# Fourteen of 22 tiles of a feed-forward's down projection as seven quarter products, eight half by half

## The reference, cut to what matters

```
gu = x @ w_gu                                  # 1024 x (2*2816)
gate, up = gu[..., :2816], gu[..., 2816:]
ffn = (silu(gate) * up) @ w_down               # (1024 x 2816) @ (2816 x 1024)
x   = layer_norm(ALPHA * x + ffn, ln2_g, ln2_b)
# second layer begins: h = rmsnorm(x, g_mix_pre) * (1 + scale_m) + shift_m ; q, k, v, ... = h @ w_in_2
```

## Time and profile before

| | us |
|---|---|
| runs (3): median | 2929.09 |
| runs: lowest, highest | 2924.64, 2931.28 |
| profiled execution | 2924.11 |
| span of its profile | 2922.4 |
| mean granted TensorE clock, of full speed | 0.992 |

### The profile page before, as it was taken

One profiled execution on the slowest core, in us unless ns is written; L12 is line 12 of the kernel. 1 busy time (PEld: TensorE's weight loads), 2 busy tenths in 40 slices (PEclk: granted clock), 3 DMA queues, 4 the chain that ended last, 5 costly groups with the idle time before them and its releaser, 6 DMA issues.

```text
span 2922.4 us, 33825 instructions
## 1 busy us (share of the span) xinstructions
PE 2827.5 (97%) x12957; PEld 2090.6 (72%) x12957; DVE 1470.3 (50%) x2344; ACT 892.4 (31%) x1532; POOL 1263.0 (43%) x824
## 2 busy tenths in 40 slices
PE   8999999889999999999899988999999899999998
PEld 5444457468888888887788655677777688888886
DVE  0599977746733334152513765221421732235998
ACT  2501036531233332112311364110121444454443
POOL 2000000036777776666667302445445587753020
PEclk9999999999999999999999999999999999999999
DMA  4111136233422224545333101333344333346864
GB/s 113 29 36 37 43 96 189 87 123 117 130 87 84 82 87 135 200 141 165 108 87 101 44 1 30 86 103 122 87 116 136 123 109 115 116 158 219 280 193 173
DMA packets 349152, 327.81 MB, mean 112 GB/s; under 512 B 17984, under 2 KB 277312, under 8 KB 348992
## 3 DMA queue, kind: packets, MB, share of 16 engines
q1 hardware_dynamic: 329664, 271.13, 31.1%
q10 hardware_dynamic: 16848, 47.39, 4.2%
q0 software_dynamic: 2480, 7.13, 0.9%
HBM read 280.41 MB, written 45.19 MB: 111 GB/s over the span
## 4 chain that ended last, share of the span: by engine, by line
PE 90%; DVE 5%; issue 2%; ACT 2%; DMA 0%; POOL 0%; ACTq 0%; DVEq 0%; SPq 0%; POOLq 0%
PE PS L1343 20%; PE PS L528 19%; PE PS L1355 13%; PE PS L844 9%; PE PS L1307 5%; PE PS L1293 4%; PE PS L1578 4%; PE PS L958 3%; PE PS L1424 2%; PE PS L976 2%; PE PS L996 2%; PE PS L1535 1%; PE PS L1397 1%; PE PS L988 1%; PE PS L1438 1%
## 5 line engine op out<-in xcount | busy, mean ns | idle before, releaser
L2753 POOL TENSOR_SCALAR w_parts<-ring 128x1024 fp32r<-128x1024 f32 x198 | 231.4, 1169 | 872.9 <-PE PS L1343 258.0
L2756 POOL TENSOR_TENSOR w_parts<-ring,w_parts 128x1024 fp32r<-128x1024 f32 x198 | 513.9, 2596 | 16.5
L1343 PE MATMUL PS<-hT_high,w_parts 128*128 128x512 f32 x1312 | 433.5, 405 | 8.7 <-DVE hT_low L2360 6.4
L587 DVE TENSOR_TENSOR arena<-arena,PS 128x512 f32<-128x512 f32 x210 | 144.5, 688 | 402.5 <-PE PS L528 401.5
L1343 PEld LDWEIGHTS PS<-hT_high,w_parts 128*128 128x128 f32 x1312 | 247.3, 188 | 71.3 <-issue 11.1
L844 PE MATMUL PS<-w_parts,hid_high 128*128 128x512 f32 x896 | 276.5, 390 | 5.7 <-DVE w_parts L809 4.1
L1343 PE MATMUL PS<-hT_low,w_parts 128*128 128x512 f32 x656 | 256.2, 391 | 0.0
L1355 PE MATMUL PS<-w_parts,hid_high 128*128 128x512 f32 x704 | 218.3, 391 | 3.9 <-DVE hid_low L629 2.2
L844 PEld LDWEIGHTS PS<-w_parts,hid_high 128*128 128x128 f32 x896 | 167.7, 188 | 42.6 <-DVE w_parts L809 6.4
L528 PE MATMUL PS<-tx_high,w_parts 128*128 128x512 f32 x576 | 183.2, 389 | 0.0
L844 PE MATMUL PS<-w_parts,hid_low 128*128 128x512 f32 x448 | 174.3, 389 | 0.0
(11 more groups left out here) (345 smaller groups left out, 5621.6 us busy)
## 6 DMA issues: line engine op xcount, KB each, us to landing
ring<-in_w_in SPq DMA_DIRECT2D x112, 512.0 KB, 3.8
arena<-hid_spill SPq DMA_DIRECT2D x172, 256.0 KB, 3.7
hid_spill<-arena ACTq DMA_DIRECT2D x54, 512.0 KB, 3.1
ring<-in_w_gu SPq DMA_DIRECT2D x52, 512.0 KB, 3.9
ring<-in_w_ada SPq DMA_DIRECT2D x48, 512.0 KB, 5.2
ring<-in_w_ff SPq DMA_DIRECT2D x96, 256.0 KB, 3.3
ring<-in_w_down SPq DMA_DIRECT2D x44, 512.0 KB, 3.6
ring<-in_w_ff SPq DMA_DIRECT2D x40, 512.0 KB, 4.0
```

Source lines behind the costliest of these rows:

```text
L587: dve.tensor_tensor(out, a, self.product(g, m), ALU.add).then_inc(self.combined, 1)
L1343: mm = pe.matmul(PS[:, 2 * p + bank, :], w[:, q, k * P:(k + 1) * P], x[:, k, half_of(h)], start=(k == order[0] and n == 0), stop=(k == ord ...
L2753: pool.tensor_scalar(w_high[:, q, :], ring[:, s, :], 1.0, 1.0, ALU.mult, ALU.mult).then_inc(weights_high, 1)
L2756: pool.tensor_tensor(w_low[:, q, :], ring[:, s, :], w_high[:, q, :].bitcast(F32), ALU.subtract).then_inc(weights_used[s], 1)
```

## The change

Tiles 0 to 13 go through a second `DownSevens` (`mul1`, n_k = 7, 49 steps, products drained into y1 by `mul1.drain`); tiles 14 to 21 go through `Down` as before (REST1 = 8 steps in each half). The residual no longer rides in the add that takes the bank: `add_rows1` adds ALPHA*x1 from a second place in SBUF to y1, eight operations after step 4, and `add_down1` then adds the bank. The work of the layer norm and RMS norm of half 0 moves to other steps. Cut to its core:

```diff
+PAIRS1 = 7
+REST1 = FT - 2 * PAIRS1
...
 ORDER += ffn_order("up1", "seven1", "turn_x1", PLAIN1, SEVENS1)
+ORDER += [("prod1", p) for p in range(7)] + [("mul1", 0)]
 for half in HALVES:
-    ORDER += [("sum1", half)] + [("down1", half * FT + k) for k in range(FT)]
+    ORDER += [("sum1", half)] + [("down1", half * REST1 + k) for k in range(REST1)]
...
 PE:
             sevens1.pe(pe, 0)
+            mul1.pe(pe)
             down1.pe(pe, 0)
...
 ACT:
-            for n in range(3, 2 * FT):
+            for n in range(3, mul1.n):
+                mul1.act(act, n)
+            for n in range(2 * REST1):
                 down1.act(act, n)
-                if n == FT + 4:
+                if n == REST1 + 5:
                     ln_sqrt_half(1, 0)
-                if n == FT + 5:
                     ln_scale_half(1, 0)
-                if n == FT + 9:
-                    for b in range(4):
-                        store_x2(b)
-                        square_sum(y1[:, b, :], b, junk)
-                    sums_done(0)
-                if n == FT + 11:
-                    rms_sqrt_half(0, 0)
-                if n == FT + 13:
-                    xhat_half(0)
+            for b in range(4):
+                store_x2(b)
+                square_sum(y1[:, b, :], b, junk)
+            sums_done(0)
+            rms_sqrt_half(0, 0)
+            xhat_half(0)
...
 DVE:
+            def add_rows1(b):
+                y = y1[:, b, :].rearrange("p (a n) -> p a n", a=2)
                 dve.wait_ge(rows_back, 16 * NB)
-                dve.scalar_tensor_tensor(out=y1[:, b, :], in0=y1[:, b, :], scalar=ALPHA, in1=flat(p),
-                                         op0=ALU.mult, op1=ALU.add).then_inc(psum_free[p], 1)
+                do(dve.scalar_tensor_tensor(out=y, in0=x1_back[b], scalar=ALPHA, in1=y, op0=ALU.mult, op1=ALU.add))
...
-            for n in range(3, 2 * FT):
+            for n in range(3, mul1.n):
+                mul1.dve(dve, n)
+                if n % PAIRS1 == 3 and n > PAIRS1:
+                    mul1.drain(dve, n // PAIRS1 - 1, y1, link)
+            for n in range(2 * REST1):
                 down1.dve(dve, n)
+                if n == 2:
+                    mul1.drain(dve, 6, y1, link)
                 if n == 4:
+                    for i in range(2):
+                        mul1.drained(dve, 6, i)
+                    for b in range(NB):
+                        add_rows1(b)
                     pool_counts()
-                if n == FT + 2:
+                if n == REST1 + 3:
                     for u in range(4):
                         add_down1(0, u)
-                if n == FT + 3:
                     for u in range(4):
                         freed(dve, "sum1", 0, u)
                     ln_stats(1, 0)
-                if n == FT + 5:
+                if n == REST1 + 5:
                     ln_gain(1, 0)
-                if n == FT + 6:
+                if n == REST1 + 6:
                     ln_gain(1, 2)
-                if n == FT + 9:
-                    rms_mean(0, 0)
-                if n == FT + 11:
-                    rms_recip(0, 0)
+            rms_mean(0, 0)
+            rms_recip(0, 0)
...
 SP:
+            for n in range(mul1.n):
+                mul1.load_weights(sp, n, t["w_down"][0], slot_free)
+                mul1.load_hidden(sp, n, hidden1)
+                b, other = divmod(n - 3 * PAIRS1, 3)
+                if 0 <= b < NB and not other:
+                    sp.dma_start(x1_back[b], x1_dram[tok(b), :].rearrange("p (a n) -> p a n", a=2)
+                                 ).then_inc(rows_back, 16)
+            for n in range(2 * REST1 + 2):
+                if n < 2 * REST1:
+                    row_tile_load("down1", n, 0, t["w_down"][0], 2 * PAIRS1 + n % REST1)
                 if n >= 2:
-                    hidden1(n - 2)
-                if n == 7:
-                    sevens1.after(sp, SEVENS1, 0)
-                    for b in range(NB):
-                        sp.dma_start(y1[:, b, :], x1_dram[tok(b), :]).then_inc(rows_back, 16)
+                    down1.sp(sp, n - 2, *stored1(2 * PAIRS1 + (n - 2) % REST1))
```

More of the change, by code:

```diff
@@ L97 @@
     "seven1": (sevens(2), []),
+    "prod1": ([], ["own", "own"]),
+    "mul1": (down_steps(PAIRS1), []),
     "sum1": ([], [None, None, None, "own"]),
@@ L135 @@
             **{(stage, i): (p,) for stage in ("turn_x1", "turn_h2") for i, p in ((4, 0), (5, 3), (6, 1), (7, 0))},
-            **{("sum2", p): (2 * (p % 2), 2 * (p % 2) + 1) for p in range(7)}}
+            ("sum1", 0): (2, 3, 0, 1), ("sum1", 1): (2, 3, 0, 1),
+            **{("turn_h", i): ((i + 2) % 4,) for i in range(4)},
+            **{(stage, p): (2 * (p % 2), 2 * (p % 2) + 1) for stage in ("prod1", "sum2") for p in range(7)}}
 class Ledger:
@@ L188, in __init__ @@
                 pairs[p] += 1
-                n_units += 1
+                n_units += stage != "prod1"
         self.fulls = fulls
@@ L605, in program, with __init__ @@
         class Down:
-            def __init__(self, stage, n0, sums, n_k, sevens, hidden, back, high, low):
-                self.stage, self.sums, self.n_k, self.sevens, self.hidden = stage, sums, n_k, sevens, hidden
+            def __init__(self, stage, n0, sums, n_k, first, before, hidden, back, high, low):
+                self.stage, self.sums, self.n_k, self.first, self.before, self.hidden = stage, sums, n_k, first, before, hidden
                 self.back, self.high, self.low = back, high, low
@@ L611, in __init__, with slot @@
                 self.n0, self.split_high, self.split_low = n0, hid_high, hid_low
+                self.moved = [before.moved0[s] + before.moved_of[s] for s in range(4)]
+            def slot(self, n):
+                return (self.n0 + n) % 4
             def sp(self, sp, n, stored, value):
                 h, k = divmod(n, self.n_k)
-                self.sevens.after(sp, self.sevens.n - 1, 4)
-                if n >= 4:
-                    sp.wait_ge(self.split_low, self.n0 + n - 3)
+                sp.wait_ge(self.split_low, self.n0 + n - 3)
@@ L618, in sp @@
                 sp.wait_ge(stored, value)
-                sp.dma_start(self.back[:, n % 4, :], self.hidden[k, :, half_of(h)]).then_inc(tile_moved[n % 4], 16)
+                sp.dma_start(self.back[:, self.slot(n), :], self.hidden[self.first + k, :, half_of(h)]
+                             ).then_inc(tile_moved[self.slot(n)], 16)
             def act(self, act, n):
-                act.wait_ge(tile_moved[n % 4], 16 * ((self.n0 + n) // 4 + 2))
+                s = self.slot(n)
+                act.wait_ge(tile_moved[s], self.moved[s] + 16 * (n // 4 + 1))
@@ L636, in product @@
                     n = h * self.n_k + k
-                    return token_product(pe, L.pair(self.sums, h, u), L.part(self.stage, n, 0), self.high, self.low, n % 4,
+                    return token_product(pe, L.pair(self.sums, h, u), L.part(self.stage, n, 0), self.high, self.low, self.slot(n),
                                          slice(u * P, (u + 1) * P), k == 0, k == last)
@@ L795, in dve @@
             def dve(self, dve, n):
+                if n == 0:
+                    self.before.after(dve, self.before.n - 1, 4)
                 self.add_hidden(dve, n + 1)
@@ L905, in drain @@
                         dve.tensor_tensor(c10, c10, bank, ALU.add).then_inc(free, 1)
+                    else:
+                        self.drained(dve, 5, i)
+                        dve.tensor_tensor(c10, c10, bank, ALU.subtract).then_inc(free, 1)
             def bank_here(self, eng, u, full):
@@ L2438, in group1 @@
                 if g == SEVENS1 - 1:
-                    down1.dve(dve, 2)
+                    mul1.dve(dve, 2)
                 sevens1.sums_here(dve, g, 7)
@@ L2839, in _ @@
                 pool.dma_start(dst, t[name].to_broadcast([P, D])).then_inc(ln_rows_loaded[1], 16)
-            for n in range(2 * FT):
+            mul1.pool(pool)
+            for n in range(2 * REST1):
                 split_weights("down1", n)
```

79 lines of the change are left out of this document (46 added, 33 removed).

## The result

The changed kernel takes 2933.67 us (median of 11 runs) where the kernel before took 2925.84 in the runs made beside it; the ratio is 1.0026, 95% interval 1.0016 to 1.0036. It is slower by some 7.6 us, with 84 matmuls fewer. The profiled execution shown here is one of the longer ones: 2937.89 us, span 2936.2.

The account below looks back on a forecast made before the run. PE was taken as the bound, busy 97% of the span and 90% of the chain. Terms -19.0 + 1.0 + 9.3 + 9.7 + 6.3 = +7.3 us on 2929.1 gave 2936.4 us, range 2918 to 2945.

Parts of the forecast that it names:

- seven products themselves: Seven products of seven steps in down1: DVE's drains every 7 steps are covered, by 2 us, so PE does not wait.
- drain of product 6: Transition to the eight-tile stage: the drain frees a pair at T+3.8, block 2 wants it at T+2.7; +1.0 us.
- residual adds, step 5: Half 0: eight two-input additions alternate with POOL, 2.7 us each, delaying low part 5; stall 7.5 us, with clock +9.3 us.
- boundary: Between the halves: bank adds stand behind a later tile's low part, PE starts at X+9.7, not X+1.8; with clock +9.7 us.
- half 1: Last two steps: low part 15 queued behind ln_gain on DVE; stall 8.3, clock 1.8, less 3.8 lost before: +6.3 us.
- rows scaled for turn_h: After half 1: RMS-norm scaling ends near X+60, just when turn_h comes after two blocks; 0, at most 3 us.
- What goes: Matmuls of 14 tiles in down1: 672 become 588, so 84 x 226.7 ns go, -19.0 us however the rest falls.
- The clock: PE, after a stall of over 2 us, runs partly at the lower of 2.4 and 1.2 GHz; 1.6 to 2.0 us more.
- third rival: Products 2, 3 and 5: PE waits 3 us in each for DVE, on top of the forecast; 2946, chance 0.10.
- light lock: Residual adds and ln_gain: DVE mostly wins over POOL, additions take 1.3 us; sum -12.1, 2917 us, chance 0.18.
- Residual adds alone covered: Half 0, step 5: the residual adds cost nothing, the rest as forecast; -2.0, 2927 us, chance 0.17.
- DVE-bound products: Seven products: drains every 19 us make PE wait in products 2, 3, 5, 3 us each; 2946 us, chance 0.10.

Follow-up runs that it names:

- half of ln_gain: Changed kernel with bank adds sooner, residual adds spread, drain sooner, and ln2_b additions left out for blocks 0 to 3: ratio 0.9930 to before, 2907.89 us.
- the three moves: Changed kernel with bank adds behind REST1+2, residual adds spread over steps 4 to 7, product 6's drain behind step 1: ratio 0.9965 to before, 2916.41 us.
- residual adds spread: Changed kernel with two residual adds behind each of steps 4 to 7 of half 0, not eight behind step 4: ratio 1.0004 to before, 2927.73 us.
- sooner bank adds: Changed kernel with half 0's four bank adds behind step REST1+2 instead of REST1+3: ratio 1.0003 to before, 2926.52 us.

## Why the prediction was right

The forecast was +7.3 us, 2936.4 in a range of 2918 to 2945; measured was a ratio of 1.0026, +7.6 us, and 2933.7. Term by term, idle times from the rows above:

| term | forecast | measured |
|---|---|---|
| fewer matmuls | 84, -19.0 | 84 by the counts: 588 + 384 for 1056 |
| seven products themselves | covered | 0.4 us idle |
| drain of product 6 | stall 1.1 | 2.3 (1.8 in other runs) |
| residual adds, step 5 | stall 7.5, clock 1.8 | 5.4, clock 2.1; 6.4 us off when spread |
| boundary | stall 9.7, of which 7.9 new, clock 1.8 | 9.5, of which 7.8 new; 6.7 us off when moved (9.8 in the stage) |
| half 1 | stall 8.3, clock 1.8 | 7.2; 10 us with its clock, by half of ln_gain |
| rows scaled for turn_h | 0 | 0 |

- *What goes* held. With the three moves and half of ln_gain the ratio is 0.9930, 20.5 us off; the 84 matmuls (19.0 us) and the 3.8 us that before lost in half 1 make 22.8, and the drain's and the entry's small waits stand against it.
- *The residual adds* were right in mechanism: 20.66 us for eight, forecast 20.4. The stall was 2.1 us too long in the forecast, since PE wants step 5 later than I had it: 31.7 us after its first matmul of the eight-tile part instead of 27.2, for the drain's 2.3 us and the lower clock after them. I had priced the drain and then not carried it on. Low part 5 was late too, done after 37.0 us instead of 34.7, as the additions began 1.5 us later and the counts' small operations took 3.53 us; the two errors partly cancel.
- *The boundary* was the sharpest term, since a row of before held the very tile: 9.7 forecast, 9.5 measured. What it costs in time is less sharp: forecast 9.7 us with the clock, 6.7 by the runs and 9.8 by the stage in the profiles.
- *Half 1* was right in mechanism: ACT's root came 17.2 us after PE resumed, as forecast (1376.9 against 1359.7), and low part 15 was the late one. The two ends of it on DVE:

```profile
1376.91 0.18 DVE L2334 RECIPROCAL misc<-misc 128x4 f32<-128x4 f32 x1 [6.44 <-ACT misc L1688]
...
1400.26 0.68 DVE L648 TENSOR_TENSOR hid_low<-arena,hid_high 128x512 fp32r<-128x512 f32 x1
```

  The four pairs of ln_gain took 5.15, 5.29, 4.55 and 5.23 us, 20.2 in all, where the forecast had eight times 2.7, 21.6; that is most of the 1.1 us by which the stall is shorter.
- *The clock* was taken at 1.6 to 2.0 us for each stall; after step 5's it was 2.1. I had it for three stalls; the drain's has it too (granted clock 0.72 in the 6 us from 1300). Nor does it take "over 2 us", as the forecast read from one row: with the residual adds spread, the drain's stall of 1.79 us is followed by a granted clock of 0.89 and 0.83 in the two windows of 6 us from 1292, while the boundary's 1.69 with the sooner bank adds left it at 1.00.
- *Two slips of the forecast* change nothing: the operation of 3.43 us that it calls an addition is ln_gain's multiplication (L2316), of the same shape and inputs, and its third rival adds up to 2945.4, not 2946.

The *light lock* rival is out: additions took 2.6 us, not 1.3. *Residual adds alone covered* is out as well: they stalled step 5 for 5.4 us. *DVE-bound products* is out: 0.4 us of idle in 133. Idle time was 24.4 us in the four places where I had 26.5 (1.4 more at the entry, in this profile), and the clock was lost four times instead of three: the agreement of the total owes something to errors that cancel, drain and clock too small, adds and half 1 too large.

## What to carry to other kernels

When a stage gets shorter, price what rides in its queues, not only its own work: four blocks of other work that were hidden in 22 steps were bare in 8, and cost more than the 19 us saved. For a block on another engine the question is how many steps lie ready when it starts, and whether its first operation stands behind a load that in turn stands behind a freed buffer: one step of delay made PE wait 7.8 us longer. Three moves in that order turned the same change from 0.26% slower to 0.35% faster.

## What I had not expected

- A stall can pay for another. One step of delay at the boundary makes a stall 7.8 us longer in both kernels, but before got 3.8 us back in half 1, and removing the drain's wait gave back only 1 of 2 us, as step 5's grew by 1.0.
- The entry of the eight-tile part varied between profiled executions of the same order of work. In the profiled execution of the changed kernel POOL's first subtraction starts just before DVE's low part of the last product step:

```profile
1286.60 2.71 POOL L2793 TENSOR_TENSOR w_parts<-ring,w_parts 128x1024 fp32r<-128x1024 f32 x1
1286.97 2.88 DVE L819 TENSOR_TENSOR hid_low<-arena,hid_high 128x512 fp32r<-128x512 f32 x1
```

  The low part takes 2.88 us instead of 0.69. The first matmul of the eight-tile part comes 136.3 us after the first of the products there (1294.95 against 1158.63), but 133.6 us in the profiles of all seven other kernels with 49 product steps, where the last product step's low part started before POOL. Of these 2.7 us, 1.4 are the idle time at the entry (the first row of the PE timeline above); the rest is small gaps inside the products, the first of them at 1246, long before POOL comes in. The order of arrival of two operations can thus be the reason for no more than a part, and it was not tried by itself: DVE was by then 2.4 us later than in the kernel with the sooner bank adds, counted from the first product, and why is open. The 2.7 us are most of the 4.2 us by which this profiled execution lies above the median.
